# Sums of squares finished by TensorE, and two tiles of the last scaling on GpSimd

## The reference

```
for l in range(2):
    h = rms_norm(x, norm1_g[l]) * (1 + sc1) + sh1
    mix = mixer(h @ w_in[l]) @ w_out[l]      # gated short convolution | retention
    x = x + g1 * mix
    h2 = rms_norm(x, norm2_g[l]) * (1 + sc2) + sh2
    x = x + g2 * (square(relu(h2 @ w_up[l])) @ w_down[l])
return rms_norm(x, final_g)                  # y = x * rsqrt(mean(x*x) + eps) * g
```

## Time and profile before

| | |
|---|---|
| three runs | 1204.19, 1205.29, 1205.61 us, median 1205.29 |
| span of the profiled execution, first to last instruction | 1202.4 us |
| TensorE busy | 1158.5 us, 96% |
| VectorE busy | 700.7 us, 58% |
| ScalarE busy | 439.7 us, 37% |
| GpSimd busy | 274.2 us, 23% |
| mean granted TensorE clock | 0.993 |

### The profile page before, as it was taken

The page is one execution under the profiler, slowest core; times in us unless marked ns, Lnnn a source line. Parts: engine busy times, 40 slices in busy tenths (PEclk is TensorE's granted clock), DMA queues, the critical chain, the costliest instruction groups (busy, mean ns, idle before and its releaser), DMA issues.

```text
span 1202.4 us, 17270 instructions
## 1 busy us (share of the span) xinstructions
PE 1158.5 (96%) x5702; PEld 978.4 (81%) x5702; DVE 700.7 (58%) x871; ACT 439.7 (37%) x620; POOL 274.2 (23%) x191
## 2 busy tenths in 40 slices
PE   2799999999999999999999999999999999999997
PEld 1688788899888888888897888889988888888886
DVE  7899877767443434443367897766764232333333
ACT  5445444335332123432243544424534212343220
POOL 4369210132110001120113940104222000112110
PEclk9899999999999999999999999999999999999998
DMA  9655434224443353343234433433353323232212
GB/s 358 259 175 179 153 108 154 101 107 160 160 141 138 105 190 125 115 147 105 87 136 158 164 140 127 138 120 123 108 192 119 105 89 103 88 105 93 98 36 72
DMA packets 46910, 161.75 MB, mean 135 GB/s; under 512 B 5520, under 2 KB 7696, under 8 KB 46736
## 3 DMA queue, kind: packets, MB, share of 16 engines
q1 hardware_dynamic: 46864, 161.13, 38.2%
HBM read 159.01 MB, written 2.10 MB: 134 GB/s over the span
## 4 chain that ended last, share of the span: by engine, by line
PE 80%; DVE 10%; issue 6%; POOL 2%; ACT 1%; DMA 0%; DVEq 0%; SPq 0%; ACTq 0%; POOLq 0%
PE ps L304 25%; PE ps L306 25%; PE ps L305 25%; DVE ada_raw L784 3%; DVE w_lo L773 2%; PE ps L484 1%; POOL buf_a L1202 1%; PE ps L469 1%; POOL buf_b L1203 1%; DVE arena L953 1%; PE ps L344 1%; DVE w_lo L989 1%; PE ps L345 1%; PE ps L346 1%; DVE ssum L944 0%
## 5 line engine op out<-in xcount | busy, mean ns | idle before, releaser
L773 DVE TENSOR_TENSOR w_lo<-w_raw,w_hi 128x1024 fp32r<-128x1024 f32 x193 | 259.4, 1346 | 300.8 <-ACT w_hi L570 298.7
L304 PE MATMUL ps<-h_hi,w_hi 128*128 128x512 f32 (+1 forms) x960 | 363.7, 379 | 3.4 <-issue 1.8
L306 PE MATMUL ps<-h_hi,w_lo 128*128 128x512 f32 (+1 forms) x960 | 360.9, 376 | 0.0
L305 PE MATMUL ps<-h_lo,w_hi 128*128 128x512 f32 (+1 forms) x960 | 360.7, 376 | 0.0
L570 ACT CAST w_hi<-w_raw 128x1024 fp32r<-128x1024 f32 x196 | 204.6, 1046 | 245.0 <-PE ps L306 230.7
L304 PEld LDWEIGHTS ps<-h_hi,w_hi 128*128 128x128 f32 x960 | 181.1, 189 | 37.2 <-issue 2.0
L304 PE MATMUL ps<-u_hi,w_hi 128*128 128x512 f32 (+1 forms) x576 | 211.0, 366 | 0.0
L305 PE MATMUL ps<-u_lo,w_hi 128*128 128x512 f32 (+1 forms) x576 | 210.5, 365 | 0.0
L306 PE MATMUL ps<-u_hi,w_lo 128*128 128x512 f32 (+1 forms) x576 | 210.5, 365 | 0.0
L306 PEld LDWEIGHTS ps<-h_hi,w_lo 128*128 128x128 f32 x960 | 181.0, 189 | 33.0
L305 PEld LDWEIGHTS ps<-h_lo,w_hi 128*128 128x128 f32 x960 | 181.1, 189 | 32.2
(11 more groups left out here) (123 smaller groups left out, 1066.7 us busy)
## 6 DMA issues: line engine op xcount, KB each, us to landing
w_raw<-weights SPq DMA_DIRECT2D x200, 512.0 KB, 3.3
ada_raw<-ada SPq DMA_DIRECT2D x80, 512.0 KB, 4.4
arena<-ada SPq DMA_DIRECT2D x16, 512.0 KB, 14.9
x<-xT SPq DMA_DIRECT2D x2, 1024.0 KB, 6.7
outT<-x SPq DMA_DIRECT2D x8, 256.0 KB, 2.3
tab<-tables SPq DMA_DIRECT2D x1, 1024.0 KB, 15.1
tab<-tables SPq DMA_DIRECT2D x1, 512.0 KB, 9.8
ident<-identity SPq DMA_DIRECT2D x1, 64.0 KB, 2.0
```

The costliest lines, as they stand in the source:

```text
L304: nc.tensor.matmul(out, wh, hi, start=first, stop=False, skip_group_check=True)
L305: nc.tensor.matmul(out, wh, lo, start=False, stop=False, skip_group_check=True)
L306: return nc.tensor.matmul(out, wl, hi, start=False, stop=last, skip_group_check=True)
L773: nc.vector.tensor_tensor(w_lo[:, j, :], w_raw[:, j, :], w_hi[:, j, :].bitcast(F32), ALU.subtract).then_inc(w_lo_done, 1)
```

## The change

Three edits. (1) The last square of each half (s = 7 and 11 for n = 1 and 3; 7 and 9 for n = 2 and 4) is no longer added to `ssum` by GpSimd. `mean_squares` waits for ScalarE's square itself and accumulates in PSUM, per block, one matmul with the block of `ssum` and one with the block of `buf_a[:, 1]`, where the last square lies. Eight GpSimd adds go, and eight calls of `mean_squares` have twice the matmuls. (2) For the final scaling of half 1, ScalarE multiplies tiles 4 and 5 by `final_g` early, and after the last `spread` TensorE spreads the same diagonal once more into another bank (O), ScalarE copies it to `buf_b`, and GpSimd multiplies the two tiles by it. VectorE has six tiles left. (3) SyncE sends the last half's pairs in the same order, (0,1), (2,3), (4,5), (6,7); the third waits for GpSimd. All the rest of the diff renumbers the semaphore counts.

```diff
@@ sync
-                for k in range(0, KT, 2):
-                    sp.wait_ge(out_ready, half * KT + k + 2)
+                ready = half * KT
+                for k in (0, 2, 4, 6) if half == 0 else (0, 2, *FINAL_POOL[:1], 6):
+                    if half and k in FINAL_POOL:
+                        sp.wait_ge(out_pool, 2)
+                    else:
+                        ready += 2
+                        sp.wait_ge(out_ready, ready)
                     sp.dma_start(outT[k:k + 2, :, at].rearrange("k p t -> p k t"), x[:, k:k + 2, at]
                                  ).then_inc(out_done, 16)
@@ tensor
-            def mean_squares(n, half, added, tiles=2):
+            def mean_squares(n, half, added, squares=None, tiles=2):
 
                 pe.wait_ge(ssum_added, added + 2)
+                if squares is not None:
+                    pe.wait_ge(sq_ready, squares)
                 for t in range(half * 2, half * 2 + tiles):
                     mm = nc.tensor.matmul(ps[:, STAT, t:t + 1], ssum[:, t * P:(t + 1) * P], mean_d[:],
-                                          start=True, stop=True, skip_group_check=True)
+                                          start=True, stop=squares is None, skip_group_check=True)
+                    if squares is not None:
+                        mm = nc.tensor.matmul(ps[:, STAT, t:t + 1], buf_a[:, 1, t * P:(t + 1) * P], mean_d[:],
+                                              start=False, stop=True, skip_group_check=True)
                 mm.then_inc(stat_ps, 1)
...
-            mean_squares(2 * DEPTH, 1, DEPTH * SQ)
+            mean_squares(2 * DEPTH, 1, DEPTH * ADD, DEPTH * SQ)
             pe.wait_ge(out_ready, KT)
             spread(2 * DEPTH, 1, HALVES[1])
+            nc.tensor.matmul(ps[:, O, HALVES[1]], ones[:], ssum[:, HALVES[1]], start=True, stop=True
+                             ).then_inc(rinv_again, 1)
@@ scalar, last layer only
                     norm_root(l * 2 + 2, 0)
+                    for k in FINAL_POOL:
+                        nc.scalar.activation(x[:, k, HALVES[1]], x[:, k, HALVES[1]], ACT.Copy, scale=fin_g[:, k:k + 1]
+                                             ).then_inc(final_gain, 1)
                     down_square(1, 0)
                     down_square(1, 1)
                     norm_root(l * 2 + 2, 1)
+                    act.wait_ge(rinv_again, 1)
+                    nc.scalar.copy(buf_b[:, 0, HALVES[1]], ps[:, O, HALVES[1]]).then_inc(final_rinv, 1)
@@ vector, final(half)
                 for k in range(KT):
+                    if half and k in FINAL_POOL:
+                        continue
@@ gpsimd
-                for s in range(SQ_MIX):
+                for i, s in enumerate(s for s in range(SQ_MIX) if s not in LAST_MIX):
...
-                for s in range(6, SQ_MLP):
+                for i, s in enumerate(s for s in range(6, SQ_MLP) if s not in LAST_MLP):
...
+            pool.wait_ge(final_rinv, 1)
+            for k in FINAL_POOL:
+                pool.wait_ge(final_gain, k - FINAL_POOL[0] + 1)
+                nc.gpsimd.tensor_tensor(x[:, k, HALVES[1]], x[:, k, HALVES[1]], buf_b[:, 0, HALVES[1]], ALU.mult
+                                        ).then_inc(out_pool, 1)
```

More of the change, by code:

```diff
@@ L45 @@
 SQ = SQ_MIX + SQ_MLP
+LAST_MIX, LAST_MLP = (7, 11), (7, 9)
+ADD_MIX, ADD_MLP = SQ_MIX - 2, SQ_MLP - 2
+ADD = ADD_MIX + ADD_MLP
+FINAL_POOL = (4, 5)
 FIRST_MODS = 2 * KT
@@ L359, in v_end, with v_step @@
                     mm.then_inc(pe_unit, 2)
-            def v_step(u, xs, n, added):
+            def v_step(u, xs, n, added, squares):
                 for units in ((0, 2), (2, 4)):
@@ L375, in v_step @@
                         if part == [0, 1]:
-                            mean_squares(n, 1, added)
+                            mean_squares(n, 1, added, squares)
                         if part == [0]:
@@ L384, in v_step, with first_step @@
                 v_end(4, (2, 3), xs + KT)
-            def first_step(u, xs, n, added):
+            def first_step(u, xs, n, added, squares):
                 def product(half, j, k):
@@ L429, in _ @@
             pe.wait_ge(x_added, KT - 1)
-            mean_squares(0, 0, 0, TOKEN_TILES)
+            mean_squares(0, 0, 0, tiles=TOKEN_TILES)
             spread(0, 1, WHOLE)
@@ L506, in _ @@
                             mm.then_inc(pe_unit, 1)
-                n, added = l * 2 + 1, l * SQ
+                n, added, squares = l * 2 + 1, l * ADD, l * SQ
                 for half in range(2):
@@ L516, in _ @@
                         if half and j == 0:
-                            mean_squares(n, 0, added + (SQ_MIX - SLOTS))
+                            mean_squares(n, 0, added + LAST_MIX[0], squares + (LAST_MIX[0] + 1))
                         if half and j == 1:
@@ L522, in _ @@
                     if half == 0:
-                        first_step(u0 + U_UP[0], xs + XS_H2, n, added + SQ_MIX)
+                        first_step(u0 + U_UP[0], xs + XS_H2, n, added + ADD_MIX, squares + SQ_MIX)
                     with pe.Fori(1 - half, 4) as i:
@@ L538, in _ @@
                                      k0=8 * kk, first=(kk == 0), last=(kk == 1))
-                n, added = l * 2 + 2, l * SQ + SQ_MIX
+                n, added, squares = l * 2 + 2, l * ADD + ADD_MIX, l * SQ + SQ_MIX
                 for half in range(2):
@@ L550, in _ @@
                             if half and m == 0 and kk == 0:
-                                mean_squares(n, 0, added + (SQ_MLP - 2))
+                                mean_squares(n, 0, added + LAST_MLP[0], squares + (LAST_MLP[0] + 1))
                             if half and m == 0 and kk == 1:
@@ L592, in high, with square @@
                                      bias=mod[:, shift:shift + 1]).then_inc(xs_hi, 1)
-            def square(added, s, xk, at=WHOLE):
-                act.wait_ge(ssum_added, added + s + 1)
+            def square(added, s, xk, at=WHOLE, last=()):
+                act.wait_ge(ssum_added, added + (2 + sum(a not in last for a in range(s - 1))))
                 nc.scalar.activation(buf_a[:, s % 2, at], xk, ACT.Square).then_inc(sq_ready, 1)
@@ L712, in _ @@
                     split_hi(l, h + 3, 3)
-                added = l * SQ
+                added = l * ADD
                 for m in range(SLOTS):
@@ L721, in out_square @@
                     act.wait_ge(evac_dve, l * ED + (2 + ED_OUT + (half + 1) * SLOTS + j + 1))
-                    square(added, (half + 1) * SLOTS + j, x[:, SLOTS + j, HALVES[half]], HALVES[half])
+                    square(added, (half + 1) * SLOTS + j, x[:, SLOTS + j, HALVES[half]], HALVES[half], LAST_MIX)
                 for j in range(SLOTS):
@@ L741, in _ @@
                                 split_hi(l, i + 13, j)
-                added = l * SQ + SQ_MIX
+                added = l * ADD + ADD_MIX
                 with act.Fori(0, 3) as i:
@@ L754, in down_square @@
                     act.wait_ge(evac_dve, l * ED + (2 + ED_DOWN[1] + 6 + half * 2 + m + 1))
-                    square(added, 6 + half * 2 + m, x[:, 6 + m, HALVES[half]], HALVES[half])
+                    square(added, 6 + half * 2 + m, x[:, 6 + m, HALVES[half]], HALVES[half], LAST_MLP)
                 for m in range(2):
```

20 lines of the change are left out of this document (11 added, 9 removed).

## The result

The changed kernel takes 1207.28 us (median of 12 runs, 1206.79 to 1208.04), the kernel before 1204.35 (12 runs, 1203.37 to 1205.61, the three of the start among them). That is +2.9 us, ratio 1.0023 with a 95% interval of 1.0015 to 1.0031, so +1.8 to +3.7 us. The kernel is slower, clear of zero, and the forecast +2.8 lies inside. The interval also holds the 0.2% (2.4 us) from which a difference was to count, so whether the change lies past that border is not settled. The median of before has itself come down from 1205.29 by 0.9, and the time forecast, 1208.1, is too high by about that much. The profiled spans are 1202.4 and 1205.2 us.

The account below looks back on a forecast made before the run. TensorE, busy 96% of the span, was taken to bound the kernel. Stream 2.2, last norm half 0.24 and final scaling 0.4 summed to +2.8 us, 1208.1 on median 1205.29; own range 1207.3 to 1209.7, 8-in-10 range 1205.9 to 1209.8.

Parts of the forecast that it names:

- Seven calls: TensorE's stream: seven mean_squares calls each get four more pieces at 0.11 us, 0.44 a call, 3.08 us together.
- rival of free pieces: TensorE's stream: added pieces hide behind their neighbours and cost nothing, sum -0.3, 1205.0 us; chance 0.10.
- sign that I gave for a call: TensorE's mean_squares calls: eight pieces, with 0.88 us from the matmul before them to the one after.
- GpSimd adds that go: VectorE's h_lo and weight splits: 0.70 us back at n = 2, half 1; 0.1 each at n = 1 and 3.
- term for n = 1 and 3: Removed last GpSimd add holds one h_lo there: at most 0.26 us back each, at least nothing, taken as 0.1 each.
- The last norm half: Last sums on TensorE: the v_step branch holds them, so 0.20 us gained, four more pieces cost 0.44: +0.24 us.
- The final scaling: Half-1 output: VectorE's 0.80 us gain is lost as the last pair queues behind GpSimd's slow pair: +0.4 us.
- The sum: Whole kernel: 2.2 (stream) + 0.24 (last norm half) + 0.4 (final scaling) = +2.8 us, giving 1208.1 us.
- lower end of the range, 1207.3: Whole kernel: low end of the forecast's own range from its terms' bounds, 1207.3 to 1209.7 us.
- bound of -0.43 for a missing branch: Last norm half: lower bound of its +0.24 us term, if no branch holds TensorE's last sums.
- third rival: Last sums: the branch does not hold them, TensorE starts at 1192.78 (0.64 better); sum +1.6, 1206.9 us; chance 0.08.
- rival of the clock drop: After layer 0's loop branch: the half-clock stretch, costing 1.7 us, does not come; sum +1.1, 1206.4 us; chance 0.13.

Follow-up runs that it names:

- experiment 1: The change with only the half-0 last squares (s = 7) on TensorE, half 1 and final scaling as in the kernel before: 1206.55 us, ratio 1.0017.
- experiment 2: The change with only the half-1 last squares (s = 11, 9) on TensorE, half 0 and final scaling as in the kernel before: 1205.46 us, ratio 1.0011.
- experiment 6: Kernel before, with last square of n = 2 and 4, half 1, on TensorE, and its last sums and spread ahead of the v_step If: 1205.32 us.
- experiment 8: experiment 6 and experiment 7 combined, with last sums and both spreads ahead of the v_step If: 1205.58 us, ratio 1.0010 to the kernel before.
- experiment 10: Kernel before with TensorE's layer loop written out and the last square of n = 2 and 4, half 1, on TensorE: 1203.83 us, ratio 0.9996.
- experiment 11: experiment 10 plus GpSimd's two final tiles, sent last, and tiles 0 and 1 sent singly: 1203.31 us, ratio 0.9992 to the kernel before.
- experiment 12: The whole change with TensorE's layer loop written out: 1205.08 us, ratio 1.0009 to the kernel before.
- experiment 3: Kernel before with only the final scaling changed (GpSimd takes tiles 4 and 5), transfer order as in the change: 1204.46 us, ratio 1.0003.
- experiment 4: experiment 3 with GpSimd's pair (4,5) sent last: 1204.66 us, ratio 1.0002 to the kernel before.
- experiment 7: experiment 4 with tiles 0 and 1 of half 1 sent singly: 1205.26 us, ratio 1.0006 to the kernel before.
- experiment 5: Kernel before with TensorE's last sums and spread in their own If ahead of v_step's, sums' adds still on GpSimd: 1205.94 us, ratio 1.0012.

## Why the prediction was right

**Seven calls.** Forecast were 3.08 us of pieces at 0.11, six calls visible at 0.44 and one hidden. The table has six steps of 0.44, and experiment 1 has them by themselves. The floor of 25 ns that the Trainium skill gives (TensorE: Matmul & The Clock Gate, "Wait — 56ns, not 53.3ns?") is not what these pieces cost: it is 0.11 us with one column, in each kernel of this case. The rival of free pieces is out. The sign that I gave for a call, 0.88 us from the matmul before it to the one after, left out the step of 0.12 ahead of the pieces; the trace has 0.93.

**GpSimd adds that go.** n = 2 gave 0.26 and hid its pieces, as forecast. The term for n = 1 and 3 was mis-sized: I took 0.1 each from a range of 0 to 0.26, it was 0.22 and 0.23 (0.19 and 0.20 in experiment 2). At n = 1 the last h_lo takes 0.48 instead of 0.74 us there, and still 0.74 in experiment 1, which keeps the add and has a step of only 0.04: TensorE does wait for that last h_lo nearly in full. The stream came to 1.93 instead of 2.2.

**The last norm half.** The step was that the branch, not the add, sets the start. Forecast +0.24, measured +0.29 (-0.13 and +0.42). The change and experiments 2, 6, 8, 10, 11 and 12 settle it, the kernels in which only the square is waited for: with the branch in front the sums start 1.85 to 2.07 us after the last product, without it 1.12 to 1.20. The rule of the Trainium skill on a taken branch (Runtime: NRT & Kernel Launch, "Instruction fetch mechanics") agrees with the trace: a branch that goes far, out of the `If` or back to the loop's start, lasts 3.4 to 4.0 us in every kernel with the loop, with a 16 KB instruction packet inside, and no such wait appears once the loop is written out.

**The final scaling.** The step was right, the size too large: +0.4 forecast, +0.22 measured, +0.20 alone in experiment 3. The copy ended 1.26 us after the first spread's end, forecast 1.28, and the two multiplies were done 1.48 us later instead of 1.60, so the third transfer left 2.77 after the spread's end (2.73 after the first scaling) and not 2.91. The fourth landed 5.74 after it, not 5.91. That the queue order does the damage is shown by experiment 4. That the whole megabyte's rate then sets the end was my theory there, and it fell in experiment 7.

**The sum.** 1.93 + 0.29 + 0.09 + 0.22 = 2.5 us stand at the places of the change, the 0.09 by the clock. That the spans differ by 2.78, so close to 2.8, is in part luck: the stream was put 0.3 and the scaling 0.2 too high, and 0.23 that no edit caused came in from the clock, besides the 0.09. The lower end of the range, 1207.3, also does not follow from the bounds as they were given: 1.9 - 0.43 - 0.03 makes +1.4, so 1206.7. The bound of -0.43 for a missing branch was left to the third rival.

**The rival of the clock drop.** It came true in its mechanism and failed in its price. In the changed kernel the stretch after the loop's branch keeps its clock, to be held against the earlier trace rows:

```profile
642.50:645.91 3.41, 3.15 (x14) 2.62 (x15) 3.37 (x5) 0.80 (x1) 0.00 (x0) 1.00 0.32 124
```

I had priced the drop at 1.7 us. Between the layers the changed kernel gains 0.59; experiments 1 and 3 to 8, which keep the loop and have no drop either, gain 0.55 to 0.65, and experiment 2, which has the drop as before, 0.01. The stage behind takes back the rest, and the traces show where. GpSimd's rotary work begins at 650.46 us in the changed kernel and at 650.74 before, so 1.95 us earlier against the +1.67 at the end of `v_step`. Its first six rounds end at 689.23, before at 688.14: only 0.58 earlier against it. Their twelve multiplies by the table take 25.6 us together instead of 24.4. Two of them are these (timelines of GpSimd, before and after):

```profile
673.16 1.31 POOL L1203 TENSOR_TENSOR buf_b<-buf_b,tab 128x512 f32<-128x512 f32 x1
678.89 1.29 POOL L1203 TENSOR_TENSOR buf_b<-buf_b,tab 128x512 f32<-128x512 f32 x1
```

```profile
672.24 2.27 POOL L1228 TENSOR_TENSOR buf_b<-buf_b,tab 128x512 f32<-128x512 f32 x1
679.01 2.28 POOL L1228 TENSOR_TENSOR buf_b<-buf_b,tab 128x512 f32<-128x512 f32 x1
```

Before, VectorE waited for ScalarE for 0.54 and 1.70 us beside these two; in the changed kernel it works through. So the earlier start costs GpSimd the moments in which it had run undisturbed. The twelve take 25.5 to 25.7 us in all kernels without the drop and 24.3 in experiment 2, which has it.

Whether the change had a part in the missing drop stays open. Experiments 3, 4 and 7 have the layer code of the kernel before and no drop, so it isn't the edit's alone. But the two executions with the drop are the earliest at the end of `v_step` (shifts 0 and +0.21); from +0.41 on there is none. The changed kernel stands at +1.67 there, half of it from the start and half from its own steps.

## What to carry to other kernels

Where an add is taken off a chain, ask what else the next engine is doing at that moment, its sequencer included: a wait that ends within 0.2 us of the one removed takes its place, and the profile then names a releaser that had long been done. Work moved into the stream of the bound engine is paid at each place it stands, while the wait it removes may exist at one place only; put it there alone. (In experiment 10 the trace has that gain; the median is too coarse to show it.) And before work at the end is split over two engines, look at the queue that carries the result out: the part that is ready last must be sent last. Even so it gained nothing here (0.03 us in experiment 4), because the last two transfers then land 0.75 us apart.

## What was not expected

**A code fetch delays the data of other queues.** In experiments 5, 6 and 8 one 16 KB instruction packet among the last 256 KB of output moved its landing from 2.2 us after the issue to 3.9, 3.7 and 4.0. Where a far branch stands decides which data it meets.

**The start differs by up to 1.7 us between executions.** The product of `y` and the output weights of layer 0, ahead of which no instruction was changed, starts at 215.58 us in the profiled run of before, at 216.40 in that of the change and at 217.25 in experiment 5. The windows from 40 to 50 us (busy of the engines, granted clock, DMA share, GB/s) of before and of experiment 5:

```profile
40.00:50.00 10.00, 8.10 (x29) 6.55 (x30) 9.86 (x20) 6.53 (x15) 0.00 (x0) 0.74 0.92 370
```

```profile
40.00:50.00 10.00, 7.67 (x21) 6.15 (x22) 9.86 (x19) 6.56 (x13) 0.27 (x1) 0.58 0.94 377
```

The clock granted is 0.74 in the one and 0.58 in the other, since it rose to 2.4 GHz at 45.2 us in the one and at 48.3 in the other. Over the fourteen traces the start of that product follows the time of this rise, from 215.6 to 217.3. In the profiled run of the change the rise came at 46.8 us, 1.66 later than before; half of that, lost at half the clock, is the table's +0.82. It may well explain much of the spread of single times, but each kernel has only one trace, so that is not shown. It is a reason to read a step of 0.2 us between two events of one trace.
